# Cross attention: the sample's probabilities and their turn in buffers of their own, and its steps moved ahead of the second unit's values

## The reference

```
def _mem_attn(h, mk, mv, w_q, q_norm, w_o):
    q = _rmsnorm((h @ w_q).reshape(bsz, t, X_HEADS, X_HEAD_DIM), q_norm)
    logits = einsum("bthd,bmhd->bhtm", q, mk).astype(float32) * (X_HEAD_DIM ** -0.5)
    probs = softmax(logits, axis=-1)
    o = einsum("bhtm,bmhd->bthd", probs, mv).reshape(bsz, t, X_HEADS * X_HEAD_DIM)
    return o @ w_o
```

## Time and profile before

| | us |
|---|---|
| median of 3 runs | 1567.85 |
| lowest, highest | 1567.64, 1569.78 |
| profiled execution, its own time | 1568.68 |
| its span in the profile | 1566.9 |
| PE busy | 1551.6 (99%) |
| DVE busy | 988.8 (63%) |
| POOL busy | 666.2 (43%) |
| ACT busy | 641.0 (41%) |

### The profile page before, as it was taken

How to read it: one execution, slowest core, us unless ns; L and a number is a source line. 1 busy time by engine, 2 the same in 40 slices (tenths; PEclk the granted TensorE clock), 3 DMA queues, 4 the chain that set the end, 5 groups by cost and what they waited for, 6 DMA issues and landing times.

```text
span 1566.9 us, 30883 instructions
## 1 busy us (share of the span) xinstructions
PE 1551.6 (99%) x11966; PEld 1489.9 (95%) x11966; DVE 988.8 (63%) x1408; ACT 641.0 (41%) x953; POOL 666.2 (43%) x317
## 2 busy tenths in 40 slices
PE   9999999999999999999999999999999999999999
PEld 8889848998999999999999998999899999999999
DVE  7798895776565564555657879757657552055530
ACT  6332464546443332333335675445543332133321
POOL 4345521461343433343435757554143334343442
PEclk9999999999999999999999999999999999999999
DMA  5343321340322232222223333334122223222222
GB/s 207 133 145 100 129 82 41 108 151 26 121 81 94 80 111 77 81 80 94 96 81 104 105 102 121 105 112 148 38 84 84 91 89 105 66 90 90 89 93 95
DMA packets 42393, 153.89 MB, mean 98 GB/s; under 512 B 5632, under 2 KB 6656, under 8 KB 41032
## 3 DMA queue, kind: packets, MB, share of 16 engines
q1 hardware_dynamic: 42312, 152.75, 28.9%
HBM read 145.53 MB, written 9.30 MB: 99 GB/s over the span
## 4 chain that ended last, share of the span: by engine, by line
PE 85%; DVE 6%; issue 3%; POOL 2%; ACT 2%; DMA 0%; POOLq 0%; SPq 0%; DVEq 0%; ACTq 0%
PE PS L1087 76%; PE AX L1087 3%; POOL WLO L508 2%; DVE TB L2086 1%; DVE SC L1689 1%; ACT PX L843 1%; PE AX L1438 1%; DVE LG L1850 1%; PE AX L1320 1%; DVE RB L2088 1%; DVE SC L1672 0%; PE PS L1333 0%; DVE M L1671 0%; PE AX L1353 0%; PE AX L1142 0%
## 5 line engine op out<-in xcount | busy, mean ns | idle before, releaser
L508 POOL TENSOR_TENSOR WLO<-WRAW,WHI 128x1024 fp32r<-128x1024 f32 (+3 forms) x301 | 635.7, 2121 | 883.8 <-ACT WHI L572 883.6
L572 ACT ACTIVATE WHI<-WRAW 128x1024 fp32r<-128x1024 f32 (+3 forms) x301 | 268.7, 913 | 580.8 <-PE PS L1087 549.6
L1087 PE MATMUL PS<-XH,WHI 128*128 128x272 f32 (+1 forms) x2128 | 443.7, 290 | 0.3 <-DVE XL L1629 0.3
L1087 PE MATMUL PS<-XH,WLO 128*128 128x272 f32 (+1 forms) x2128 | 440.0, 288 | 0.0
L1087 PE MATMUL PS<-XL,WHI 128*128 128x272 f32 (+1 forms) x2128 | 437.7, 287 | 0.0
L1087 PEld LDWEIGHTS PS<-XH,WHI 128*128 128x128 f32 x2128 | 337.2, 188 | 7.8 <-issue 3.7
L1087 PEld LDWEIGHTS PS<-XL,WHI 128*128 128x128 f32 x2128 | 337.1, 188 | 0.0
L1087 PEld LDWEIGHTS PS<-XH,WLO 128*128 128x128 f32 x2128 | 335.2, 188 | 0.0
L1087 PE MATMUL PS<-HH,WHI 128*128 128x272 f32 x1216 | 252.5, 289 | 0.1
L1087 PE MATMUL PS<-HH,WLO 128*128 128x272 f32 x1216 | 251.2, 288 | 0.0
L1087 PE MATMUL PS<-HL,WHI 128*128 128x272 f32 x1216 | 251.2, 288 | 0.0
(11 more groups left out here) (322 smaller groups left out, 1852.5 us busy)
## 6 DMA issues: line engine op xcount, KB each, us to landing
WRAW<-in_w_in_even SPq DMA_DIRECT2D x29, 512.0 KB, 3.3
WRAW<-in_w_up0a SPq DMA_DIRECT2D x22, 512.0 KB, 3.2
WRAW<-in_w_up0b SPq DMA_DIRECT2D x22, 512.0 KB, 3.2
WRAW<-in_w_up1a SPq DMA_DIRECT2D x22, 512.0 KB, 3.2
WRAW<-in_w_up1b SPq DMA_DIRECT2D x22, 512.0 KB, 3.2
WRAW<-in_w_mv SPq DMA_DIRECT2D x16, 512.0 KB, 3.3
WRAW<-in_w_xq SPq DMA_DIRECT2D x16, 512.0 KB, 3.3
WRAW<-in_w_xo SPq DMA_DIRECT2D x16, 512.0 KB, 3.3
```

What stands on the lines that cost most here:

```text
L508: pool.tensor_tensor(WLO[parity][:, first:last], WRAW[parity][:, first:last], WHIf[parity][:, first:last], ALU.subtract).then_inc(lo_done, ...
L572: act.activation(WHI[parity][:, first:last], WRAW[parity][:, first:last], ACT.Copy).then_inc(hi_done, 2 // len(cuts))
L1087: ins = pe.matmul(dst, w, x, start=first, stop=last)
```

## The change

The sample's probabilities move from PX1 to the scratch buffer SQ, and its turned probabilities from AX to a free half of PSUM bank PS[:, 1, 0], whose other half holds the sample's logits. The other units keep PX0 (s = 0, 2) and PX1 (s = 1, 4). The waits follow: exponentials(3) wait for no turn, exponentials(4) for turn(1), and turn(3) waits for unit 1's exponentials (which read the bank before) and no longer for AX to be read. On PE turn(3) goes ahead of values(1). On ACT exponentials(3) go ahead of the weight chunk `ahead(c0 + 7)`, and turned(3) ahead of exponentials(4). On DVE maximum(3) goes ahead of low_part(0), and normalise(3) ahead of maximum(4).

```
+        def cross_probs(s):
+            return SQ[:, 0, 0:MEM].unsqueeze(1) if XUNITS[s] == 4 else (PX0, PX1)[s in (1, 4)]
-        SAMPLE_ROWS = PS[:, 1, 1, 0:256]
+        SAMPLE_ROWS, SAMPLE_TURNED = PS[:, 1, 1, 0:256], PS[:, 1, 0, 256:512]
...
                 def exponentials(s):
-                    nq, px = (P if XUNITS[s] < 4 else SAMPLE), (PX0, PX1)[s % 2]
+                    nq, px = (P if XUNITS[s] < 4 else SAMPLE), cross_probs(s)
                     act.wait_ge(xnm, b + s + 1)
-                    if s >= 2:
-                        act.wait_ge(xt_done, b + s - 1)
+                    if s in (2, 4):
+                        act.wait_ge(xt_done, b + s // 2)
...
-                        act.activation(PTXS[:], AX[:, 0, 0:256], ACT.Copy).then_inc(xt_read, 1)
+                        act.activation(PTXS[:], SAMPLE_TURNED, ACT.Copy).then_inc(xt_read, 1)
...
                 turned(1)
+                exponentials(3)
                 ahead(c0 + 7)
-                exponentials(3)
                 turned(2)
+                turned(3)
                 exponentials(4)
-                turned(3)
                 high_part(1)
...
                 def turn(s):
-                    px = (PX0, PX1)[s % 2]
+                    px = cross_probs(s)
                     pe.wait_ge(xp, b + s + 1)
-                    if s:
+                    if s == 3:
+                        pe.wait_ge(xexp, 4 * (b + 2))
+                    elif s:
                         pe.wait_ge(xt_read, b + s)
                         pe.wait_ge(xt_low, 4 * l + TURNS_SPLIT[s])
...
-                                ins = pe.transpose(AX[:, 0, P * mb:P * mb + P], px[:, 0, P * mb:P * mb + P], IDENT)
+                                ins = pe.transpose(SAMPLE_TURNED[:, P * mb:P * mb + P], px[:, 0, P * mb:P * mb + P], IDENT)
...
                 turn(2)
+                turn(3)
                 values(1)
-                turn(3)
                 sample_values(3)
...
                 normalise(2)
+                maximum(3)
                 low_part(0)
                 turned_low(1)
-                maximum(3)
+                normalise(3)
                 maximum(4)
-                normalise(3)
                 turned_low(2)
```

## The result

| | us |
|---|---|
| changed kernel, median of 22 runs | 1571.77 (1571.32 to 1572.77) |
| kernel before, median of 22 runs beside them | 1568.02 (1566.91 to 1571.23) |
| ratio | 1.0024, 95% interval 1.0018 to 1.0030 |
| profiled execution of the changed kernel, its own time and span | 1572.32, 1570.5 |

The change makes the kernel 3.75 us slower; 3.86 was forecast.

A forecast was written before the change was run, and what follows sets the result against it. TensorE (PE) was taken to bound the kernel, so only its idle time in cross attention counts: +1.93 us a layer, +3.86 in all, on the 1567.85 us median gave 1571.7 us, range 1569.3 to 1572.8.

The forecast's parts named there:

- Buffers at 0: Cross attention: sample's probabilities in SQ and turned columns in PSUM cost nothing, bound 0 to 0.1 us.
- maximum(3), 0.58 us on turn(2): DVE: maximum(3) ahead of low_part(0) delays turned_low(1), and so turn(2) on PE, by 0.58 us.
- The block: DVE: the sample's multiplication falls under POOL's subtraction, ending 0.15 us after it instead of taking 0.35; chance 0.77.
- rival without the block: DVE: multiplication takes 0.35 us under POOL, leaving only the DVE delay: +0.85 us a layer, +1.7 in all; chance 0.13.
- The signs: Trace: multiplication about 2.0 us, turn(3) waiting over 1 us, turn(4) near 375.65, no sample_values(3) wait, among others.
- The Trainium skill's rule: SBUF port pair: of a two-port tensor_scalar and a GpSimd instruction, the second blocks until the first finishes; literally, 370.64.
- The rival of the stalls that go: PE: early sample turn frees ACT, winning up to 1.2 us idle a layer: -2.4 us, 1565.5 us; chance 0.05.

The follow-up runs named there:

- e1: Kernel before with only the change's buffers and waits, all three engine orders left as before: ratio 1.0000, turn(1) to turn(4) 9.80 us, as before.
- e2: Kernel before with one edit, maximum(3) ahead of low_part(0) on DVE: ratio 1.0005, turn(1) to turn(4) 10.39 us, +0.59 a layer.
- e8: The changed kernel timed again, nothing altered: ratio 1.0018, 1571.73 us against 1568.24 before; turn(1) to turn(4) 11.67 us.
- e4: Changed kernel with the weight chunk's rounding on ACT back ahead of exponentials(3): ratio 1.0011, turn(1) to turn(4) 10.96 us, +1.16 against before.
- e3: Changed kernel with the weight chunk's rounding on ACT moved behind sample_rows: ratio 1.0006, turn(1) to turn(4) 10.66 us, +0.86 against before.
- e5: Changed kernel with the sample's multiplication on ACT instead of DVE: ratio 1.0009, turn(1) to turn(4) 10.67 us, +0.87 against before.
- candidate: Change's buffers, PE and ACT orders of before, DVE: maximum(3), turned_low(1), low_part(0), maximum(4), normalise(3), turned_low(2): ratios 0.9998 and 0.9995 against before.
- e7: First run of the change's buffers with PE and ACT orders of before and maximum(3), turned_low(1) first on DVE: ratio 0.9998, 1567.98 us.

## Why the prediction was right

Step by step, as distances in us from the start of turn(1) (363.92 in the trace that the forecast was made from, 363.77 in the one after):

| step | forecast | measured |
|---|---|---|
| turned_low(1) begins | 3.19 | 3.19 |
| turn(2) begins | 4.55 | 4.55 |
| POOL's subtraction | 3.98 to 6.37 | 3.98 to 6.33 |
| the sample's multiplication | 4.51 to 6.52 | 4.51 to 6.49 |
| turn(3) begins | 6.57 | 6.54 |
| maximum(4) begins | 6.46 | 6.41 |
| exponentials(4) begin | 7.92 | 7.85 |
| turn(4) begins | 11.73 | 11.67 |

- **Buffers at 0.** Right, and shown by e1: no cost and no gain.
- **maximum(3), 0.58 us on turn(2).** Right in kind and size, shown alone by e2 (+0.59).
- **The block.** Right: forecast to end 0.15 after POOL, it ended 0.16 after (0.14 in e8). e4 gives the same 0.15 with another overlap, e3 and e5 take the block away by two different means and leave +0.86 and +0.87. So the sum of a layer is 0.86 for the orders and 1.01 for the block; the forecast had 0.85 (its rival without the block) and the rest of 1.93, 1.08. The excess of 0.07 is about half POOL's subtraction, 2.35 us where I had 2.39 from the row before; two hand-overs, from the multiplication to maximum(4) and from there to exponentials(4), were 0.02 shorter each.
- **The signs.** All came but one in size: turn(3) was to wait over 1 us, and the trace lists 0.93, counted from the modelled end of turn(2).
- **The Trainium skill's rule** (SBUF — State Buffer, Who interferes with whom): the full block holds here, in two lengths. Its literal reading, the whole 0.35 us only after POOL's end, does not: 0.14 to 0.16 us was left.
- **The rival without the block** (+1.7) is what e3 and e5 measured in the trace, so its price was right and its condition was not met. **The rival of the stalls that go** needed turn(2) not later than before; it was 0.58 later. One part of it came true all the same: sample_values(3) no longer waits for ACT's copy. That was worth nothing, because turn(4) behind it hung on exponentials(4), which the change put off.

Not tried: turn(3) ahead of values(1) on PE alone. That this order costs nothing by itself is read from e3, where turn(3) did not wait and turn(4) hung on DVE, and is not shown by a run of its own. Nor was that order tried with the candidate's DVE list.

## What to carry to other kernels

Before giving a step a buffer of its own, look at what released it last: here it was the order of another engine's list, and the buffer was worth nothing (e1). When a step moves on one engine, follow what it issues on others: 0.7 us later on ACT for the rounding moved a GpSimd instruction of 2.4 us fully over a VectorE instruction of 0.35 us, which had itself moved ahead under its end; the meeting cost 1.01 us a layer (0.30 by the VectorE step's move and 0.71 more by GpSimd's), more than the orders themselves (0.86). A step moved ahead in a list without a gap delays all that stands between its new place and its old one by its full length, however short it is (e2).

## What the runs showed of the hardware

- A VectorE tensor_scalar, fp32, 256 columns in SBUF, that starts while a GpSimd subtraction on SBUF is under way ends 0.14 to 0.16 us after that one has ended (1.98 us in the changed kernel, 1.97 in e8 and 1.26 in e4, in place of 0.35). The same on ScalarE under the same subtraction took 0.51 us (e5).
- A VectorE tensor_tensor of only 4 columns with both inputs in SBUF is held as well: 0.74 in place of 0.16 us, ending 0.02 after POOL (e5). Subtractions with one input in PSUM were not held (1.21 us partly under POOL in the kernel before, 1.22 wholly under it in e7), and neither was a tensor_scalar of one column (0.21 us).
